# V rows of a tile one stage later, sub keys folded into the query weights, mixer in three PSUM banks

## What is computed

```
q = (hf @ w_q).reshape(t, 8, 2, 128)                  # hf = RMSNorm(x), t tokens
scores = einsum('thpd,pkd->thpk', q, sub_keys)        # 8 heads x 2 halves x 128 keys
s1, i1 = top_k(scores[:, :, 0], 16); s2, i2 = top_k(scores[:, :, 1], 16)
top_s, top_c = top_k(s1[.., :, None] + s2[.., None, :], 16)
idx = e1 * 128 + e2; gates = softmax(top_s)           # 128 experts a token
act = gelu(einsum('td,tkd->tk', hf, u_tab[idx]))
y = einsum('tk,tkd->td', gates * act, v_tab[idx])
out = RMSNorm(x + y)
```

## Time and profile before

| what | value |
|---|---|
| median of 3 runs | 3587.24 us (3586.83 to 3588.61) |
| profiled execution, its own time | 3575.1 us |
| span of the profile | 3573.5 us |
| TensorE, VectorE, GpSimd, ScalarE busy | 73%, 58%, 57%, 9% |
| moved by DMA | 1159.13 MB, 324 GB/s over the span |
| gathers | 2048 of 512 KB: 1024 for U, 1024 for V |

### The profile page before, as it was taken

How to read it: one execution, slowest core, us unless ns; L and a number is a source line. 1 busy time by engine, 2 the same in 40 slices (tenths; PEclk the granted TensorE clock), 3 DMA queues, 4 the chain that set the end, 5 groups by cost and what they waited for, 6 DMA issues and landing times.

```text
span 3573.5 us, 30245 instructions
## 1 busy us (share of the span) xinstructions
PE 2597.0 (73%) x8914; PEld 1022.7 (29%) x8914; DVE 2078.7 (58%) x4579; ACT 334.7 (9%) x705; POOL 2038.3 (57%) x2109
## 2 busy tenths in 40 slices
PE   7999956157857785778578857785778677765588
PEld 4444543143123212321232124212321232110121
DVE  3332032879478647865686567755875586646600
ACT  2221011001001100010001000100110011000000
POOL 1100000346766776677667766775677667777765
PEclk8999978568979997899799979897999789976699
DMA  3334320579999999999999999999999999999998
GB/s 101 106 112 148 132 80 0 208 241 393 352 388 375 409 366 373 375 410 366 369 374 409 368 384 358 410 367 360 377 410 375 373 372 409 362 396 410 409 399 349
DMA packets 351628, 1159.13 MB, mean 324 GB/s; under 512 B 43280, under 2 KB 72848, under 8 KB 350480
## 3 DMA queue, kind: packets, MB, share of 16 engines
q0 software_dynamic: 301024, 1094.89, 79.3%
q1 hardware_dynamic: 46256, 58.69, 4.9%
q10 hardware_dynamic: 4224, 4.35, 0.3%
HBM read 1128.37 MB, written 29.43 MB: 324 GB/s over the span
## 4 chain that ended last, share of the span: by engine, by line
DMA 32%; PE 16%; DVE 15%; issue 14%; POOL 9%; ACT 1%; SPq 0%; POOLq 0%; DVEq 0%; ACTq 0%
DMA ring<-in_peer_v_dram,picks_T 12%; DMA ring<-in_peer_v_dram,at_T 10%; DMA ring<-in_peer_u_dram,picks 9%; DVE ring L1180 9%; POOL ring L794 9%; PE y_psum L838 8%; PE tile_psum L901 1%; PE tile_psum L908 1%; PE tile_psum L974 1%; PE tile_psum L907 1%; DVE arena L1262 1%; PE tile_psum L865 1%; PE tile_psum L956 1%; ACT arena L1083 1%; DVE arena L1306 1%
## 5 line engine op out<-in xcount | busy, mean ns | idle before, releaser
L838 PE MATMUL y_psum<-ring,spread 128*32 128x512 f32 x4096 | 1365.2, 678 | 502.8 <-DMA ring<-in_peer_v_dram,at_T 401.3
L1180 DVE CUSTOM_DVE_ANT_0 ring<-ring,h_psum 128x1024 f32<-128x1024 f32 x1024 | 1224.7, 1219 | 368.1 <-DMA ring<-in_peer_u_dram,picks 321.8
L794 POOL DMA_INDIRECT ring<-in_peer_u_dram,picks x1024 | 965.7, 943 | 803.2 <-DVE picks L1419 314.1
L838 PEld LDWEIGHTS y_psum<-ring,spread 128*32 128x32 f32 x4096 | 279.3, 117 | 1494.6 <-DMA ring<-in_peer_v_dram,at_T 637.3
L794 POOL DMA_INDIRECT ring<-in_peer_v_dram,picks_T x544 | 579.1, 1064 | 196.8 <-issue 130.5
L794 POOL DMA_INDIRECT ring<-in_peer_v_dram,at_T x480 | 452.3, 942 | 202.9 <-issue 121.1
L324 PE MATMUL proj<-hn_T,w_blk 128*128 128x512 f32 x640 | 280.1, 597 | 1.3 <-DVE hn_T L453 1.3
L974 PE MATMUL tile_psum<-w_q,arena 128*128 128x512 f32 x512 | 235.2, 612 | 8.8 <-ACT arena L1119 8.8
L324 PEld LDWEIGHTS proj<-hn_T,w_blk 128*128 128x128 f32 x640 | 121.2, 192 | 146.9 <-issue 145.2
L1444 DVE SCALAR_TENSOR_TENSOR h_psum<-x,stat,h_psum 128x1024 f32<-128x1024 f32 x8 | 10.3, 1290 | 257.0 <-PE h_psum L847 257.0
L974 PEld LDWEIGHTS tile_psum<-w_q,arena 128*128 128x128 f32 x512 | 96.3, 194 | 145.3 <-issue 134.3
(11 more groups left out here) (217 smaller groups left out, 2228.9 us busy)
## 6 DMA issues: line engine op xcount, KB each, us to landing
ring<-in_peer_u_dram,picks POOLq DMA_INDIRECT x1024, 7.1
...
```

What stands on the lines that cost most here:

```text
L794: pool.indirect_dma_start(ring[:, j], None, tables[kind], bass.IndirectOffsetOnAxis(ap=at, axis=0)).then_inc(filled[j], 16)
L838: last = nc.tensor.matmul(y_ps[quad * STEPS:(quad + 1) * STEPS, half], lines[:, quad, at:at + STEPS], ring[:, j, half * BANK:(half + 1) * ...
L1180: nc.vector.tensor_tensor_reduce(out=ring[:, j], in0=ring[:, j], in1=h_ps[:], scale=1.0, scalar=0.0, op0=ALU.mult, op1=ALU.add, accum_out= ...
```

## The change

1. **V rows.** All 128 V rows of tile e - 1 are now items of the stage of tile e, mixed with its U rows by two tables (`U_MARKS`, `V_MARKS`; `SEGMENTS` is 59). After the last U row come the turned picks (`T`), the copy of the picks that frees GpSimd (`K`), `G`, `C`, the weighted h (`H`), V rows 120 to 127, and `E`, `F`, `R`, `E`, `O`, `S`. body(1, 0) thus has U rows alone, and body(None, 8) all 128 V rows of tile 7. `A` (VectorE) copies `picks_T` to `at_T`, which GpSimd did before. The gates are copied to `coef` ahead of time. The unrolled loop over rounds on TensorE is gone, and the ring's slots are numbered so that the rounds come out even.
2. **Sub keys.** The host hands over `w_q` and the sub keys in another layout (no arithmetic). During tile 0's mixer TensorE multiplies each of 16 blocks of `w_q_T` with its keys, and VectorE scales the product with the norm weights and writes it to `w_q` (item `W`, `FOLD_MARKS`: 16 folds over the first 26 shares). The first ten blocks are loaded into the ring by SP ahead of tile 0's mixer inputs. The scores are then one product `h_T @ w_q`. The front stage no longer loads `w_q`.
3. **Three banks.** `tile_psum` has 3 banks, not 4. In the mixer, the SSD group's output and state now come before the doubling loop; the decay rows come in two parts; four copies of 512 take the scores out of PSUM instead of one of 2048.
4. **Norms.** h for the queries is x2 times its inverse root mean square, by ScalarE; the weights stand in `w_q`. The final norm's weights lie in SBUF as a row (`final_row`), and the result has a tile of its own (`res`). The scratch for DMA descriptors is set to 8192 bytes.

```diff
+SEGMENTS = 59
+U_MARKS = ((0, 0), (1, PRELUDE), (22, 66), (28, 80), (37, 112), (SEGMENTS, 120), (SEGMENTS + 1, PICKS))
+V_MARKS = ((0, 0), (1, 0), (26, 52), (29, 58), (37, 58), (SEGMENTS, 104), (SEGMENTS + 1, P - TAIL))
+FOLD_MARKS = ((0, 0), (26, LISTS), (SEGMENTS + 1, LISTS))
...
+    for u_end, v_end in zip(share_ends(U_MARKS), share_ends(V_MARKS, 2)):
+        u0, v0 = u, v
+        while v < v_end:
+            pick(u0 + (u_end - u0) * (v + 1 - v0) // (v_end - v0))
             seq += [("V", v, 1), ("V", v + 1, 1)]
-            for k in range(n, to):
-                seq.append(("U", k, 0))
-                if k == 9:
-                    seq += [("P", 0, 0), ("X", 0, 0)]
-            n = to
-            for b in range(EARLY_SPREADS, N_SPREADS):
...
-                    sp.dma_start(w_q[:, some], w_q_src[:, some]).then_inc(w_late_loaded, 16)
...
-        bank = ps("tile_psum", [P, 4, BANK])
+        bank = ps("tile_psum", [P, 3, BANK])
...
+                if e is None:
+                    for l in range(SLOTS):
+                        sp.dma_start(ring[:, l], A["w_q_T"][l]).then_inc(s["wq_first"], 16)
...
+                    for l in range(SLOTS, LISTS):
+                        sp.wait_ge(s["wq_ready"], l - SLOTS + 1)
+                        sp.dma_start(ring[:, l - SLOTS], A["w_q_T"][l]).then_inc(s["wq_rest"], 16)
...
-                    if item == ("V", 2 * SLOTS, 0):
-                        pool.wait_ge(s["picks_T_ready"], e + 1)
-                        pool.sem_inc(s["held"])
-                        nc.gpsimd.tensor_copy(at_T[:], picks_T[:]).then_inc(s["at_ready"], 1)
-                    if item == ("V", FRONT, 1):
+                    if item == ("V", 0, 1):
                         pool.wait_ge(s["at_ready"], e)
-                        pool.sem_inc(s["held"])
-                    if item == ("V", 0, 0):
-                        pool.wait_ge(s["picks_T_ready"], e + 1)
                         pool.sem_inc(s["held"])
                     if kind == "U":
                         at = picks[:, n:n + 1]
...
+                if kind == "W":
+                    if n < SLOTS:
+                        pe.wait_ge(s["wq_first"], 16 * SLOTS)
+                    else:
+                        pe.wait_ge(s["wq_rest"], 16 * (LISTS - SLOTS))
+                    if n >= 2:
+                        pe.wait_ge(s["wq_copied"], n - 1)
+                    for k in range(KD):
+                        last = nc.tensor.matmul(folded(n)[:, k], ring[:, n % SLOTS, k * P:(k + 1) * P], keys_T[:, n % 2], start=True, stop=True)
+                    last.then_inc(s["wq_ready"], 1)
...
+                    if n == 1:
+                        pe.wait_ge(s["y_part"], 2 * m + 1)
+                        pe.wait_ge(s["x_end_ready"], m + 1)
+                        for g in range(SSD_G):
+                            half = slice(g * SSD_R * SSD_P, (g + 1) * SSD_R * SSD_P)
+                            group = slice(g * SSD_R, (g + 1) * SSD_R)
+                            last = nc.tensor.matmul(bank[:, 2, half], tok[:, TOK_B + g * P:TOK_B + (g + 1) * P],
+                                                    x_end[:, group].rearrange("p h w -> p (h w)"), start=True, stop=True)
+                        last.then_inc(s["bx_ready"], 1)
+                        pe.wait_ge(s["y_part"], 2 * (m + 1))
+                        pe.wait_ge(s["S_ssd_ready"], m + 1)
                     pe.wait_ge(s["MX_copied"], (NL - 1) * m + n)
...
-                row_of(0, bank[:, 0:2].rearrange("p b w -> p (b w)")).then_inc(s["ffn_row_ready"], 1)
...
+                if isinstance(m, int) and m == 0:
+                    pe.wait_ge(s["wq_copied"], LISTS)
                 for b in range(4):
+                    if b == 3:
+                        pe.wait_ge(s["score_copied"], 4 * m + 1)
                     for k in range(KD):
-                        last = nc.tensor.matmul(bank[:, b], h_T[:, k], w_q[:, k, b * BANK:(b + 1) * BANK],
+                        last = nc.tensor.matmul(bank[:, SCORE_BANKS[b]], h_T[:, k], w_q[:, k, b * BANK:(b + 1) * BANK],
                                                 start=(k == 0), stop=(k == KD - 1))
                         if k == KD - 1:
-                            last.then_inc(s["q_ready"], 1)
+                            last.then_inc(s["score_ready"], 1)
                         if k % 4 == 3:
...
-                    pe.wait_ge(s["q_copied"], 4 * m + b + 1)
-                    for n in range(4):
-                        last = nc.tensor.transpose(square(b)[:, n], q[:, b % 2, n], ident[:])
-                    last.then_inc(s["q_turned"], 1)
-                    pe.wait_ge(s["qT_copied"], 4 * m + b + 1)
-                    for n in range(4):
-                        last = nc.tensor.matmul(square(b)[:, n], q_T[:, b % 2, n], keys_T[:, n % 2], start=True, stop=True)
-                    last.then_inc(s["score_ready"], 1)
...
+                nc.scalar.activation(h2, x2[:], ACT.Copy, scale=stat[:, 5:6]).then_inc(s["h2_ready"], 1)
...
+                if kind == "W":
+                    dve.wait_ge(s["wq_ready"], n + 1)
+                    tt(w_q[:, :, n * P:(n + 1) * P], folded(n), over_free(w_cols[:], P), ALU.mult).then_inc(s["wq_copied"], 1)
...
+                if kind == "K" and not last_tile(e):
+                    pass_picks(e + 1)
...
+                if kind == "H" and not last_tile(e):
+                    weigh_h(e + 1)
+                if kind == "A":
+                    dve.wait_ge(s["picks_T_ready"], e)
+                    for j in range(SLOTS):
+                        dve.wait_ge(used[j], uses_before(j, e) + 1)
+                    nc.vector.tensor_copy(at_T[:], picks_T[:]).then_inc(s["at_ready"], 1)
...
+                    nc.vector.tensor_copy(coef[:], gates[:].rearrange("p h k -> p (h k)")).then_inc(s["gates_passed"], 1)
...
+                tt(y_ssd, heads(2, SSD_H, SSD_P), over_free(e_in[:, 0:SSD_H], SSD_P), ALU.mult).then_inc(s["y_part"], 1)
+                tt(S_ssd[:], S_ssd[:], over_free(e_all[:, 0:SSD_H], SSD_P), ALU.mult).then_inc(s["S_ssd_part"], 1)
+                dve.wait_ge(s["y_part"], 2 * m + 1)
+                tt(y_ssd, y_ssd, heads(0, SSD_H, SSD_P), ALU.add).then_inc(s["y_part"], 1)
+                dve.wait_ge(s["bx_ready"], m + 1)
+                dve.wait_ge(s["S_ssd_part"], 3 * m + 1)
+                tt(S_ssd[:], S_ssd[:], heads(2, SSD_H, SSD_P), ALU.add).then_inc(s["S_ssd_ready"], 1)
+                tt(y_skip, xs, over_free(d_head[:], SSD_P), ALU.mult).then_inc(s["S_ssd_part"], 1)
+                dve.wait_ge(s["S_ssd_part"], 3 * m + 2)
+                dve.wait_ge(s["y_part"], 2 * (m + 1))
+                tt(y_ssd, y_ssd, y_skip, ALU.add).then_inc(s["S_ssd_part"], 1)
+                dve.wait_ge(s["S_ssd_part"], 3 * (m + 1))
+                tt(y_ssd, y_ssd, view(zgs[:, 0:SSD_W], SSD_H, SSD_P), ALU.mult).then_inc(s["y_gated"], 1)
...
+    nc = _bacc.Bacc("TRN2", target_bir_lowering=False, num_devices=1, dynamic_dma_scratch_size=8192)
...
+    laid_out = {"keys_T": _np.asarray(keys)[0].transpose(2, 0, 1),
+                "w_q_T": _np.asarray(w_q)[0].T.reshape(LISTS, P, D)}
```

373 lines of the change are left out of this document (171 added, 202 removed).

## The result

The changed kernel takes 3663.17 us (median of 4 runs, 3654.12 to 3675.33), the kernel before 3587.93 beside it (3586.83 to 3592.15): ratio 1.0211, 95% interval 1.0184 to 1.0237. The forecast was 3609, +0.6%, so the sign was right and the size was not. The profiled execution took 3664.39 us, its span is 3662.7.

What follows compares the result with a forecast made beforehand. The prediction took DMA gathers as the bound, with a full stage's floor at 335 us. It summed 705 + 270 + 6 x 351 + 514 = 3595, +21.5 on the span, giving a median of 3609; range 3550 to 3665.

Steps and rivals of the forecast that it cites:

- Before the first gather: Start up to the first U gather: loads +10.2, folds and SSD +41, queries -10.6, so 705.3 us instead of 664.7.
- The 41: Tile 0's mixer: sixteen folds in series cost 44.5 us, SSD out of the end gives 3.3 back; bounds 10 and 56.
- the rival with the nesting folds: Tile 0's folds fit into idle shares: +15 instead of +41 us, median 3583, no change; chance 0.12.
- First stage: First loop stage, now U rows alone: 270 us instead of 315.5, giving back 45; bounds 262 and 285.
- The mixer's term: First stage, from the mixer to the x2 add: 132 us with 60 U rows, before 138 with 69; bounds 127 and 138.
- Full stages: Six full loop stages: floor 335 plus 7, 6 and 3 is 351 us each, against 361.2, giving back 61 us.
- Blocked issues, 7: Full stage: four gather issues held by VectorE's 3.5 us operations with two SBUF inputs stay, 7 us; bounds 0 and 9.3.
- Mixer, 6: Full stage's mixer: 3 us for its start at half clock, 3 for TensorE's wait for S_ssd_ready; bounds 0 and 12.8.
- Turn, 3: Turn of a full stage: VectorE some 19 us without a U row; DMA loses 2 to 6 us, taken as 3.
- The end: Last stage's first gather to the end: 384 gathers instead of 314, 514 us instead of 425.9, costing 88.
- The loop gains nothing: Rival: TensorE's in-order waits with more V rows behind them keep stages at 361 us; median 3667; chance 0.14.
- 3555: Median of the rival where the loop reaches its floor: 344 us a stage, first gather at 695, faster; chance 0.28.

Runs made afterwards that it cites:

- e5_no_fold: Changed kernel with w_q_T loaded straight into w_q and the sixteen folds left out; 3931.59 us (one run, slow chip), first gather at 671.7 us.
- h2_end_one: Changed kernel with the last stage's V gathers reading picks_T, and rank and cand_id in the free PSUM bank; 3608.12 us, ratio 1.0066 to the kernel before (fast chip).
- e2_ssd_back: Changed kernel with the mixer's SSD part put back behind the doubling loop, in four PSUM banks; 3995.8 us, ratio 1.0122 to the kernel before (slow chip).
- g2_spread: Kernel of h2_end_one with the last three SSD operations on VectorE moved behind the loop's first share of U rows; 3960.07 us, ratio 0.9951 (slow chip).
- f1_half_u: Changed kernel with each U row's product on VectorE over only 512 of 1024 columns; 3592.34 us (one run, fast chip), full stages 353.9 us.
- h3_tail4: Kernel of h2_end_one with four V rows instead of eight between last U row and F; 3594.39 us, ratio 1.0036 to the kernel before (fast chip).
- group 4: Runs on one slow chip beside the kernel before (3979.37 us): the kernels of h2_end_one and h3_tail4, and g2_spread; h3_tail4's kernel took 3935.57 us there.

## Why the prediction was right in sign and wrong in size

- **Before the first gather: right**: 11.8, 38.8 and -10.8 for 10.2, 41 and -10.6. That the sum is right to 0.3 us is luck, as +1.6 and -2.2 nearly cancel. The 41 was 44.5 for the folds less 3.3 for the SSD part out of the end. e5_no_fold gives 39.0 for the folds alone, and a mixer without them as long as before: the folds were 5.5 too dear, and the 3.3 did not come. That they stand in series and do not nest in idle shares held; the rival with the nesting folds is out.
- **First stage: right direction**, 261.2 for 270, 9 us too dear. The mixer's term is the one: 120.8 for 132, outside its bounds of 127 to 138. The start took 30.4 for 22: "it starts as before" left out that the new order puts 16 U rows (`PRELUDE`) ahead of the first mixer operation on VectorE, where the trace before has ten.
- **Full stages: this step failed.** "Sum 335 + 7 + 6 + 3 = 351 a stage" has the right floor and three terms too small: the blocked issues lost 9.4, the mixer 10.2 and the turn 5.5, and 0.7 went under the top-k. Their sum of 25.8 instead of 16 gives the 10 us a stage, 60 in all. The stage of before lost about 27, so hardly any of the 11 us that were to come back did.
  - *Blocked issues, 7:* taken over from one window of before, with an upper bound of 9.3. The four issues of the stage from 1681.0 take 4.08, 3.22, 4.02 and 3.22 us, 10.8 over four of 0.94; in the stage of before that was read they took 3.08, 3.23, 4.26 and 3.22, 10.0 over, so the upper bound was too low as well. In h2_end_one their window lost 7.8 us less and a stage was 6.8 us shorter. The Trainium skill (SBUF — State Buffer, "Who interferes with whom") says that a VectorE instruction with two SBUF inputs contends with a GpSimd instruction that reads SBUF; the runs agree, as the issues became short while the operations stayed 3.49 us.
  - *Mixer, 6:* the prediction took 3 for the start at the lower clock, 3 for the wait for S_ssd_ready and "0 elsewhere". The window with that wait lost 9.7 us in 40. Moving the SSD part does take a dip behind the loop away (e2_ssd_back, which puts it back, costs 5 us a stage). But the dip ahead of the loop is still there in e2_ssd_back, without that wait, and unchanged in g2_spread, which breaks the stretch of VectorE operations up by three. Both are from slow chips; as far as they go, neither the wait nor the stretch is borne out as the cause. With half of VectorE's work on U rows left out the window loses 3.8 less (f1_half_u). What makes the remaining 5.9 is open, and this is the largest of the three misses.
  - *Turn, 3:* the 19 us without a U row were 26.2: the tail of V rows took 12.4 instead of 9.3, since SyncE's loads now run beside it (that they are why is argued, not shown), and the 4.7 us at the loop's branch were left out, though the trace before has them. h3_tail4 gives 3.2 a stage back.
- **The end: a wait overlooked.** The forecast allowed "1 for the refill". A is in VectorE's order behind F and O, and only the last stage has no U gathers to issue meanwhile: 18.17 us. With picks_T read directly the end is 516.7 in h2_end_one, 13.8 less, and 2.7 from the 514 of the forecast.
- **Rivals.** "The loop gains nothing" (361 a stage, 3667 us) is what happened, to 4 us, and it had a chance of 0.14. Its mechanism, TensorE's waits with V rows behind them, is at most one of three: the blocked issues and the turn together lost 14.9 us of the stage, the mixer 10.2. The range of 3550 to 3665 holds the time only because it reaches to this rival. (The rivals' medians of 3555, 3667 and 3583 lie 12 to 14 us above their spans, where the main sum adds 14; by its rule the first two are 3557 and 3669.)

With both repairs and the shorter tail the loop is at 351.0 a stage. That this is the forecast's figure is luck: the blocked issues, which the forecast kept, are gone, and the mixer's loss, which it halved, is still there (8.4 us in h3_tail4's window). The kernel still takes 1.0036 of the time before on a fast chip. There it beats the changed kernel, whose ratio was 1.0211 on another such chip, but not the one before; in group 4 its ratio is 0.9878. What stays is the bill of the design, in h3_tail4's own windows: 40.5 us before the first gather and 86.9 at the end (512.8 against 425.9), against 54.6 from the first stage and 61.7 from the loop.

Open: what makes the mixer's dip; why the gathers' rate is lower on some chips (there GpSimd has the `remote` waits), and why the loss shrinks there from 2.1% to 0.4%; no trace of the kernel before was had from one.
